# Differential attention heads on one core: three bank pairs for scores, transposes and values one round later, squares per job

## The chip, the cores and the metric

One core of one Trainium2 chip runs the whole program. The metric is the device time of one execution in microseconds (us). A core has TensorE (PE in the profile; its weight loads are PEld), VectorE (DVE), ScalarE (ACT), GpSimd (POOL) and SyncE (SP, which issues most of the DMAs). Each engine works through its own queue in order, and engines are held to one another by semaphores: an instruction may wait until a counter has reached a value, and may raise a counter when it is done.

## The reference, cut to what matters

The program is a stack of layers; the change lies in one of them, the mixer with differential attention (mixer_c), and there in what stands between the projections to q, k and v and the output projection. There are 8 heads, 512 queries, 768 keys (512 latent and 256 context) and two score maps (c = 0, 1) per head, all in fp32:

```
s = einsum('bqhcd,bkhcd->bhcqk', qi, k) * scale          # two maps a head, d = 64
p = softmax(s, axis=-1)
a = p[:, :, 0] - lam * p[:, :, 1]
o = einsum('bhqk,bkhe->bqhe', a, v)                      # e = 128
o = rms_norm(o, subln) * (1 - lam_init)                  # over e, per query and head
return o.reshape(...) @ w_out
```

## The kernel before, in words

The third part of the program runs four stages one after the other on every engine: CIn (projections; L2325), CHeads (the attention; L2444), COut (the norm over e, the transposes and the output projection; L2559) and Moe (experts, whose weights stream in by DMA). A stage's place in the code gives each engine's queue in order; SP issues the expert weights only after the output projection has been added to the residual (the wait on self.before.over(sp) in Moe.sp).

CHeads has 32 jobs, one for each head and block of 128 queries (job n is head n // 4, block n % 4). The order of work on each engine is written out by rounds(): in round n every part (delay, what) gets job n - delay. PSUM (the tile ps) has 8 banks of 512 fp32 columns.

- TensorE (CHeads.pe), round n: the scores of job n (4 matmuls in the source, 2 column segments of 384 for each of the two maps, 8 MATMUL instructions of 64x384 in the trace) into banks 0 and 1 for map 0, 2 and 3 for map 1; then the values of job n - 2 (6 matmuls accumulated, 12 instructions) into bank 6 or 7; then the transposes of job n - 1 (3 into bank 4, 3 into bank 5). All L196 are scores or values, all L202 transposes. The scores wait until both exponentials of job n - 1 are done: they reuse the same banks. The helpers mm and turn4 stand at L192 to L203.
- VectorE (CHeads.dve), round n: the mix of job n - 1 (two reciprocals L2532 and L2533, a product L2535, P0 + factor * P1 over 768 columns L2537), then for each map of job n the row maximum (L2541) and its negative (L2543), then the copy of the first three transposed blocks of job n - 1 (L2548), then the scaled output row of job n - 2 (L2552).
- ScalarE (CHeads.act), round n: the copy of the last three transposed blocks of job n - 1 (L2514), then the two exponentials of job n, 128x768 each (L2521), with their row sums.

After the last job, COut squares the whole of OT at once on ScalarE (L2587), sums the squares (VectorE L2599), takes mean plus eps (L2601), the root (L2589), the reciprocal (L2603) and scales OT at once (L2606). Only then TensorE transposes OT (8 groups of 4, L202), ScalarE (L2592) and VectorE (L2609) take the groups in turn to SBUF with the gain, and OutProj.pe multiplies (L196).

The two waits that order TensorE against the other engines in a round are these:

```
if what == "scores":
    if n:
        pe.wait_ge(self.expd, 2 * n)
...
pe.wait_ge(self.mixed, 4 * n + 4)      # before the transposes of job n
```

Of the kernel before, what the change touches and what calls it, by code (L numbers as in the profile page):

```python
# [2443 lines left out]
class CHeads:  # L2444

    SCALE = 64 ** -0.5

    def __init__(self, K, into):  # L2450
# [3 lines left out]
        self.P = [K.take(T) for _ in range(4)]  # L2454
        self.PT = [K.take(6, 128) for _ in range(2)]
        self.small = [K.take(8) for _ in range(12)]
# [3 lines left out]
        self.pt0, self.pt1 = s["ch_pt0"], s["ch_pt1"]  # L2460

    def scores_at(self, c):
        return self.K.ps[:, 2 * c:2 * c + 2, 0:384]

    def exps(self, n, c):
        return self.P[(2 * n + c) % 4]

    def nums(self, n, c):
        return self.small[(2 * n + c) % 12]

    def rounds(self, parts):

        for n in range(34):
            for delay, what in parts:
                if 0 <= n - delay < 32:
                    yield what, n - delay

    def pe(self, pe):
        K, ps = self.K, self.K.ps
        self.into.over(pe)  # L2480
        for what, n in self.rounds(((0, "scores"), (2, "value"), (1, "turn"))):
            h, qb = divmod(n, 4)
            if what == "scores":
                if n:
                    pe.wait_ge(self.expd, 2 * n)
                for j, (a, w) in enumerate(SEGS):
                    for c in range(2):
                        rows = slice(64 * c, 64 * c + 64)
                        ins = mm(pe, ps[:, 2 * c + j, 0:w], [(self.into.Qs[rows, h, qb * 128:(qb + 1) * 128], self.into.Ks[rows, h, a:a + w])])
                        if j:  # L2490
                            ins.then_inc(self.scored, 1)
            elif what == "value":
                pe.wait_ge(self.pt0, n + 1)
                pe.wait_ge(self.pt1, n + 1)
                if n >= 2:
                    pe.wait_ge(self.out, n - 1)
                mm(pe, ps[:, 6 + n % 2, 0:128], [(self.PT[n % 2][:, kt, :], self.into.VV[:, kt, 128 * h:128 * h + 128]) for kt in range(6)]
                   ).then_inc(self.valued, 1)
            else:
                pe.wait_ge(self.mixed, 4 * n + 4)  # L2500
                for half in range(2):
                    if n:
                        pe.wait_ge((self.pt0, self.pt1)[half], n)
                    turn4(pe, ps[:, 4 + half, :], [self.exps(n, 0)[:, c * 128:(c + 1) * 128] for c in range(3 * half, 3 * half + 3)], K.C("ident")
                          ).then_inc(self.turned, 1)

    def act(self, act):
        ps = self.K.ps
        for what, n in self.rounds(((1, "turned"), (0, "exp"))):
            if what == "turned":  # L2510
                act.wait_ge(self.turned, 2 * n + 2)
                if n >= 2:
                    act.wait_ge(self.valued, n - 1)
                act.activation(self.PT[n % 2][:, 3:6, :], ps[:, 5, 0:384].rearrange("p (c t) -> p c t", t=128), ACT.Copy).then_inc(self.pt1, 1)  # L2514
            else:
                for c in range(2):
                    sm = self.nums(n, c)
                    act.wait_ge(self.max, 4 * n + 2 * c + 2)
                    if n >= 2:
                        act.wait_ge(self.turned, 2 * n - 2)  # L2520
                    act.activation(self.exps(n, c).rearrange("p (s n) -> p s n", n=384), self.scores_at(c), ACT.Exp, bias=sm[:, 0:1],  # L2521
                                   scale=self.SCALE, accum_out=sm[:, 1:2]).then_inc(self.expd, 1)

    def dve(self, dve):
        ps = self.K.ps
        self.into.over(dve)
        for what, n in self.rounds(((1, "mix"), (0, "max"), (1, "turned"), (2, "out"))):
            s0, s1 = self.nums(n, 0), self.nums(n, 1)
            if what == "mix":
                P0, P1 = self.exps(n, 0), self.exps(n, 1)  # L2530
                dve.wait_ge(self.expd, 2 * n + 2)
                dve.reciprocal(s1[:, 1:2], s1[:, 1:2]).then_inc(self.mixed, 1)  # L2532
                dve.reciprocal(s0[:, 2:3], s0[:, 1:2]).then_inc(self.mixed, 1)  # L2533
# [919 lines left out]
```

## Time and profile before

| | |
|---|---|
| median of 3 runs | 4707.38 us (4703.64 to 4708.06) |
| the profiled execution | 4702.54 us, its span 4700.7 us |
| mean granted TensorE clock | 0.91 |
| busy share of the span | PE 84%, PEld 48%, DVE 35%, ACT 28%, POOL 5% |
| the attention of this layer, first score matmul to last output row | 3703.59 to 3925.02 us of the span |
| from there to the first matmul of the output projection | to 3944.93 us |
| costliest lines of the program | L196 PE 1841.9 us busy, L2626 PE 1033.8, L572 PE 463.0 |

The busy shares are averages over a dozen stages with different limits; the stage that the change touches is less than a twentieth of the span. It has to be read by itself: the chain of waits tells which wait ends last there, the timeline how one round goes.

### The profile page before, as it was taken

The page shows a single profiled execution, that of the slowest core. Times are in us where ns is not written, and L with a number is a line of the kernel's source. Part 1 is how long each engine was busy: PE and PEld are TensorE (multiplying, and loading weights), DVE is VectorE, ACT ScalarE, POOL GpSimd, SP SyncE. Part 2 cuts the span into 40 slices and gives each one's busy share as a digit, 9 for nine tenths or more (in the row PEclk, how much of TensorE's full clock was granted, in tenths as well). Part 3 has the DMA queues.
Part 4 walks back from the last instruction along what each step waited for, and adds up shares of the span by engine and source line. Part 5 has one row for each costly group of instructions (what it writes and reads, how often), then busy time and mean ns, then how long its engine had stood idle before and what let it go on. Part 6 is the DMA issues. An engine that isn't in the chain of part 4 may idle for free. (4 is left out here: it accounts for less than half of the span.)

```text
span 4700.7 us, 76675 instructions
## 1 busy us (share of the span) xinstructions
PE 3932.8 (84%) x32256; PEld 2271.8 (48%) x32256; DVE 1628.5 (35%) x4139; ACT 1312.2 (28%) x2871; POOL 227.4 (5%) x221
## 2 busy tenths in 40 slices
PE   5998577777786999998879959999879867699996
PEld 2554466666664546664657643333245444333332
DVE  2001466666672113432365221111132363211112
ACT  2000234444442123324434212222135232122221
POOL 0000000000000000101100010000011000100000
PEclk7999699899997999999868969999989988799998
DMA  5221544443432200002100059999832000699996
GB/s 198 88 73 43 146 114 118 116 114 112 120 107 80 103 10 1 19 19 78 53 1 1 1 186 355 381 382 381 297 130 65 36 1 1 236 382 378 380 377 255
DMA packets 450872, 697.55 MB, mean 148 GB/s; under 512 B 168762, under 2 KB 191448, under 8 KB 450008
## 3 DMA queue, kind: packets, MB, share of 16 engines
q1 hardware_dynamic: 428600, 613.83, 38.0%
q0 software_dynamic: 14752, 53.53, 3.4%
q10 hardware_dynamic: 7168, 25.17, 1.4%
q8 instruction: 261, 4.28, 0.4%
q14 instruction: 91, 0.75, 0.1%
HBM read 625.57 MB, written 64.54 MB: 147 GB/s over the span
## 5 line engine op out<-in xcount | busy, mean ns | idle before, releaser
L196 PE MATMUL ps<-arena 128*128 128x384 f32 (+9 forms) x6718 | 1841.9, 451 | 266.8 <-ACT arena L2521 73.8
L196 PEld LDWEIGHTS ps<-arena 128*128 128x128 f32 (+3 forms) x6718 | 1099.8, 204 | 980.6 <-issue 524.2
L2626 PE MATMUL ps<-arena 128*32 128x512 f32 x9216 | 1033.8, 602 | 47.0 <-DMA arena<-in_w 42.3
L2626 PEld LDWEIGHTS ps<-arena 128*32 128x32 f32 x9216 | 307.0, 110 | 676.0 <-issue 659.3
L572 PE MATMUL ps<-arena 64*64 64x64 f32 (+1 forms) x10624 | 463.0, 241 | 182.0 <-DVE arena L1133 63.2
L572 PEld LDWEIGHTS ps<-arena 64*64 64x64 f32 x10624 | 414.3, 146 | 262.6 <-issue 102.7
L202 PE MATMUL ps<-arena 128*128 128x128 f32 x1248 | 208.2, 308 | 121.6 <-DVE arena L3028 44.5
L2760 DVE COPY arena<-ps 128x384 f32<-128x384 f32 x64 | 35.7, 558 | 675.5 <-PE ps L2685 675.5
L202 PEld LDWEIGHTS ps<-arena 128*128 128x128 f32 x1248 | 167.2, 167 | 138.2 <-DVE arena L3028 47.9
L2736 ACT ACTIVATE arena<-ps 96x512 f32<-96x512 f32 x64 | 38.0, 594 | 650.0 <-PE ps L2626 650.0
L545 DVE SCALAR_TENSOR_TENSOR arena<-arena 128x768 f32<-128x768 f32 x48 | 45.1, 1011 | 350.4 <-PE ps L196 350.4
L386 DVE SCALAR_TENSOR_TENSOR arena<-ps,arena 128x512 f32<-128x512 f32 (+1 forms) x48 | 31.8, 662 | 307.6 <-PE ps L196 307.6
L513 ACT ACTIVATE arena<-ps 128x384 f32<-128x384 f32 x64 | 31.4, 491 | 352.5 <-PE ps L196 352.5
L2778 DVE TENSOR_TENSOR arena<-ps,arena 64x512 f32<-64x512 f32 x64 | 43.7, 682 | 226.4 <-ACT arena L2748 226.4
L1464 DVE TENSOR_REDUCE arena<-ps 128x1 f32<-128x768 f32 x64 | 61.3, 958 | 159.8 <-PE ps L196 159.8
L901 PE MATMUL ps<-arena 64*64 64x64 f32 x2304 | 103.6, 248 | 14.9 <-DVE arena L1215 11.0
L2748 ACT ACTIVATE arena<-ps 64x512 f32<-64x512 f32 x64 | 38.1, 595 | 244.4 <-PE ps L2626 244.4
L330 PE MATMUL ps<-arena 128*128 128x512 f32 (+1 forms) x208 | 87.7, 587 | 20.5 <-ACT arena L321 20.5
L2791 POOL DMA_INDIRECT arena<-htok,arena x64 | 57.8, 904 | 955.5 <-PE ps L2685 948.5
L901 PEld LDWEIGHTS ps<-arena 64*64 64x64 f32 x2304 | 91.2, 160 | 25.3 <-DVE arena L1215 17.3
L247 ACT ACTIVATE arena<-arena 128x768 f32<-128x768 f32 (+1 forms) x32 | 24.5, 785 | 254.8 <-DVE arena L386 254.8
L2541 DVE TENSOR_REDUCE arena<-ps 128x1 f32<-128x768 f32 x64 | 61.0, 953 | 88.8 <-PE ps L196 87.4
(280 smaller groups left out, 3472.8 us busy)
## 6 DMA issues: line engine op xcount, KB each, us to landing
arena<-in_w SPq DMA_DIRECT2D x192, 2048.0 KB, 22.5
arena<-in_w_mod SPq DMA_DIRECT2D x24, 2048.0 KB, 9.0
arena<-in_mod_w SPq DMA_DIRECT2D x12, 2048.0 KB, 15.3
yb<-arena ACTq DMA_DIRECT2D x64, 384.0 KB, 6.3
arena<-in_rwkv_w_in SPq DMA_DIRECT2D x8, 2048.0 KB, 10.6
rkvg<-arena POOLq DMA_DIRECT2D x32, 384.0 KB, 2.6
arena<-rkvg SPq DMA_DIRECT2D x32, 384.0 KB, 4.1
arena<-di SPq DMA_DIRECT2D x192, 64.0 KB, 2.6
```

The lines of the kernel that those rows point to most:

```text
L196: ins = pe.matmul(out, l, r, start=(i == 0), stop=(i == len(pairs) - 1))
L202: ins = pe.transpose(bank[:, i * 128:(i + 1) * 128], src, ident)
L330: ins = pe.matmul(out, w[:, k, :], self.H[:, k, a:a + n], start=(k == 0), stop=(k == KT - 1), skip_group_check=True)
L545: dve.scalar_tensor_tensor(LP[:, k, :], XX[:, k, :], K.PR("mu")[:, 8 * j + k:8 * j + k + 1], H[:, k, :], ALU.mult, ALU.add).then_inc(s["in ...
L572: ins = pe.matmul(out[p, :], l[p, :], r[p, :], start=(i == 0), stop=(i == len(pairs) - 1))
L901: ins = pe.matmul(out[p, :], src[p, :], ident[p, p], start=True, stop=True)
L1464: dve.tensor_reduce(mx, src, AX.XY if masks is None else AX.X, ALU.max).then_inc(self.max, 1)
L2541: dve.tensor_reduce(sm[:, 0:1], self.scores_at(c), AX.XY, ALU.max).then_inc(self.max, 1)
L2626: return pe.matmul(bank[32 * at:32 * at + 32, :], left[:, k, 32 * g:32 * g + 32], right[:, k, :], start=first, stop=last)
L2748: act.activation(YS[0:64, 512:1024], ps[64:128, 7, :], ACT.Copy).then_inc(self.y0, 1)
L2778: dve.tensor_tensor(YS[0:64, 512:1024], ps[0:64, 7, :], YS[0:64, 512:1024], ALU.add).then_inc(self.y1, 1)
L2791: pool.indirect_dma_start(out=moe.HG[i % 3][0:ROWS, :], out_offset=None, in_=self.K.scr["htok"][0:moe.nt, :], in_offset=bass.IndirectOffse ...
```

## The change

Six things are done to CHeads and COut.

- Scores get three pairs of banks, 0 to 5; map c of job n takes pair (2n + c) % 3. Scores of job n wait for 2n - 1 exponentials, where it was 2n.
- The transposes of a job go to banks 6 and 7, columns 0 to 383, and the values to columns 384 to 511 of bank 6 or 7. Transposes of job n now wait, for n > 0, until the transposed copy of job n - 1 (ch_pt) and the output row of job n - 1 (ch_out) are done.
- Transposes come 2 rounds behind the scores (before 1), values 3 (before 2), and the values stand ahead of the scores in TensorE's round. There are 36 rounds, before 34.
- ScalarE takes all six transposed blocks in one copy, behind the exponentials of the round; VectorE's copy (L2548) is gone. VectorE's round is maximum, mix, output row; the two reciprocals are one of two columns.
- ScalarE squares each output row of 128 columns when it is there, 4 rounds behind the scores, with the row sum as accumulator output. The big square and the big sum of COut are gone, the next stage waits for 32 squares.
- COut scales OT in four parts, one for each query block, and TensorE starts to transpose a block when its part is scaled.

The diff, with comments and blank lines cut:

```
--- before.py
+++ after.py
@@ -2445,115 +2445,117 @@
 
 
 
     SCALE = 64 ** -0.5
+    JOBS = 32
 
     def __init__(self, K, into):
         self.K, self.s, self.into = K, K.s, into
         K.top = into.inner
         self.OT = K.take(4, D)
-        self.P = [K.take(T) for _ in range(4)]
+        self.P = [[K.take(T) for _ in range(2)] for _ in range(3)]
         self.PT = [K.take(6, 128) for _ in range(2)]
-        self.small = [K.take(8) for _ in range(12)]
+        self.small = [K.take(8) for _ in range(8)]
+        self.SS, self.junk = K.take(4, 8), K.take(128)
         s = K.s
         self.scored, self.turned, self.valued = s["ch_scored"], s["ch_turned"], s["ch_valued"]
         self.max, self.expd, self.mixed, self.out = s["ch_max"], s["ch_exp"], s["ch_mixed"], s["ch_out"]
-        self.pt0, self.pt1 = s["ch_pt0"], s["ch_pt1"]
-    def scores_at(self, c):
-        return self.K.ps[:, 2 * c:2 * c + 2, 0:384]
-    def exps(self, n, c):
-        return self.P[(2 * n + c) % 4]
-    def nums(self, n, c):
-        return self.small[(2 * n + c) % 12]
+        self.pt, self.squared = s["ch_pt"], s["ch_squared"]
+    def scores_at(self, n, c):
+        b = 2 * ((2 * n + c) % 3)
+        return self.K.ps[:, b:b + 2, 0:384]
+    def values_at(self, n):
+        return self.K.ps[:, 6 + n % 2, 384:512]
+    def rows(self, n):
+        h, qb = divmod(n, 4)
+        return self.OT[:, qb, 128 * h:128 * h + 128]
 
     def rounds(self, parts):
 
-        for n in range(34):
+        for n in range(self.JOBS + 4):
             for delay, what in parts:
-                if 0 <= n - delay < 32:
+                if 0 <= n - delay < self.JOBS:
                     yield what, n - delay
 
     def pe(self, pe):
         K, ps = self.K, self.K.ps
         self.into.over(pe)
-        for what, n in self.rounds(((0, "scores"), (2, "value"), (1, "turn"))):
+        for what, n in self.rounds(((3, "value"), (0, "scores"), (2, "turn"))):
             h, qb = divmod(n, 4)
             if what == "scores":
-                if n:
-                    pe.wait_ge(self.expd, 2 * n)
+                if n >= 1:
+                    pe.wait_ge(self.expd, 2 * n - 1)
                 for j, (a, w) in enumerate(SEGS):
                     for c in range(2):
                         rows = slice(64 * c, 64 * c + 64)
-                        ins = mm(pe, ps[:, 2 * c + j, 0:w], [(self.into.Qs[rows, h, qb * 128:(qb + 1) * 128], self.into.Ks[rows, h, a:a + w])])
+                        ins = mm(pe, self.scores_at(n, c)[:, j, :], [(self.into.Qs[rows, h, qb * 128:(qb + 1) * 128], self.into.Ks[rows, h, a:a + w])])
                         if j:
                             ins.then_inc(self.scored, 1)
             elif what == "value":
-                pe.wait_ge(self.pt0, n + 1)
-                pe.wait_ge(self.pt1, n + 1)
-                if n >= 2:
-                    pe.wait_ge(self.out, n - 1)
-                mm(pe, ps[:, 6 + n % 2, 0:128], [(self.PT[n % 2][:, kt, :], self.into.VV[:, kt, 128 * h:128 * h + 128]) for kt in range(6)]
+                pe.wait_ge(self.pt, n + 1)
+                mm(pe, self.values_at(n), [(self.PT[n % 2][:, kt, :], self.into.VV[:, kt, 128 * h:128 * h + 128]) for kt in range(6)]
                    ).then_inc(self.valued, 1)
             else:
-                pe.wait_ge(self.mixed, 4 * n + 4)
+                pe.wait_ge(self.mixed, 3 * n + 3)
+                if n:
+                    pe.wait_ge(self.pt, n)
+                    pe.wait_ge(self.out, n)
                 for half in range(2):
-                    if n:
-                        pe.wait_ge((self.pt0, self.pt1)[half], n)
-                    turn4(pe, ps[:, 4 + half, :], [self.exps(n, 0)[:, c * 128:(c + 1) * 128] for c in range(3 * half, 3 * half + 3)], K.C("ident")
-                          ).then_inc(self.turned, 1)
+                    ins = turn4(pe, ps[:, 6 + half, :], [self.P[n % 3][0][:, c * 128:(c + 1) * 128] for c in range(3 * half, 3 * half + 3)], K.C("ident"))
+                ins.then_inc(self.turned, 1)
 
     def act(self, act):
         ps = self.K.ps
-        for what, n in self.rounds(((1, "turned"), (0, "exp"))):
+        self.into.over(act)
+        for what, n in self.rounds(((0, "exp"), (2, "turned"), (4, "square"))):
             if what == "turned":
-                act.wait_ge(self.turned, 2 * n + 2)
+                act.wait_ge(self.turned, n + 1)
                 if n >= 2:
                     act.wait_ge(self.valued, n - 1)
-                act.activation(self.PT[n % 2][:, 3:6, :], ps[:, 5, 0:384].rearrange("p (c t) -> p c t", t=128), ACT.Copy).then_inc(self.pt1, 1)
-            else:
+                act.activation(self.PT[n % 2].rearrange("p (j c) t -> p j (c t)", j=2), ps[:, 6:8, 0:384], ACT.Copy).then_inc(self.pt, 1)
+            elif what == "exp":
+                sm = self.small[n % 8]
                 for c in range(2):
-                    sm = self.nums(n, c)
                     act.wait_ge(self.max, 4 * n + 2 * c + 2)
-                    if n >= 2:
-                        act.wait_ge(self.turned, 2 * n - 2)
-                    act.activation(self.exps(n, c).rearrange("p (s n) -> p s n", n=384), self.scores_at(c), ACT.Exp, bias=sm[:, 0:1],
-                                   scale=self.SCALE, accum_out=sm[:, 1:2]).then_inc(self.expd, 1)
-    def dve(self, dve):
-        ps = self.K.ps
-        self.into.over(dve)
-        for what, n in self.rounds(((1, "mix"), (0, "max"), (1, "turned"), (2, "out"))):
-            s0, s1 = self.nums(n, 0), self.nums(n, 1)
-            if what == "mix":
-                P0, P1 = self.exps(n, 0), self.exps(n, 1)
-                dve.wait_ge(self.expd, 2 * n + 2)
-                dve.reciprocal(s1[:, 1:2], s1[:, 1:2]).then_inc(self.mixed, 1)
-                dve.reciprocal(s0[:, 2:3], s0[:, 1:2]).then_inc(self.mixed, 1)
-                dve.wait_ge(self.mixed, 4 * n + 1)
-                dve.tensor_scalar(s1[:, 2:3], s1[:, 1:2], s0[:, 1:2], self.into.lam[:, 4:5], ALU.mult, ALU.mult).then_inc(self.mixed, 1)
-                dve.wait_ge(self.mixed, 4 * n + 3)
-                dve.scalar_tensor_tensor(P0, P1, s1[:, 2:3], P0, ALU.mult, ALU.add).then_inc(self.mixed, 1)
-            elif what == "max":
-                for c, sm in enumerate((s0, s1)):
-                    dve.wait_ge(self.scored, 2 * n + c + 1)
-                    dve.tensor_reduce(sm[:, 0:1], self.scores_at(c), AX.XY, ALU.max).then_inc(self.max, 1)
-                    dve.wait_ge(self.max, 4 * n + 2 * c + 1)
-                    dve.tensor_scalar(sm[:, 0:1], sm[:, 0:1], -self.SCALE, None, ALU.mult).then_inc(self.max, 1)
-            elif what == "turned":
-                dve.wait_ge(self.turned, 2 * n + 1)
-                if n >= 2:
-                    dve.wait_ge(self.valued, n - 1)
-                dve.tensor_copy(self.PT[n % 2][:, 0:3, :], ps[:, 4, 0:384].rearrange("p (c t) -> p c t", t=128)).then_inc(self.pt0, 1)
+                    if n >= 3:
+                        act.wait_ge(self.turned, n - 2)
+                    act.activation(self.P[n % 3][c].rearrange("p (s n) -> p s n", n=384), self.scores_at(n, c), ACT.Exp, bias=sm[:, c:c + 1],
+                                   scale=self.SCALE, accum_out=sm[:, 2 + c:3 + c]).then_inc(self.expd, 1)
             else:
                 h, qb = divmod(n, 4)
+                act.wait_ge(self.out, n + 1)
+                if n:
+                    act.wait_ge(self.squared, n)
+                act.activation(self.junk, self.rows(n), ACT.Square, accum_out=self.SS[:, qb, h:h + 1]).then_inc(self.squared, 1)
+    def dve(self, dve):
+        self.into.over(dve)
+        for what, n in self.rounds(((0, "max"), (1, "mix"), (3, "out"))):
+            sm = self.small[n % 8]
+            if what == "mix":
+                P0, P1 = self.P[n % 3]
+                dve.wait_ge(self.expd, 2 * n + 2)
+                dve.reciprocal(sm[:, 4:6], sm[:, 2:4]).then_inc(self.mixed, 1)
+                dve.wait_ge(self.mixed, 3 * n + 1)
+                dve.tensor_scalar(sm[:, 6:7], sm[:, 5:6], sm[:, 2:3], self.into.lam[:, 4:5], ALU.mult, ALU.mult).then_inc(self.mixed, 1)
+                dve.wait_ge(self.mixed, 3 * n + 2)
+                dve.scalar_tensor_tensor(P0, P1, sm[:, 6:7], P0, ALU.mult, ALU.add).then_inc(self.mixed, 1)
+            elif what == "max":
+                for c in range(2):
+                    dve.wait_ge(self.scored, 2 * n + c + 1)
+                    dve.tensor_reduce(sm[:, c:c + 1], self.scores_at(n, c), AX.XY, ALU.max).then_inc(self.max, 1)
+                    dve.wait_ge(self.max, 4 * n + 2 * c + 1)
+                    dve.tensor_scalar(sm[:, c:c + 1], sm[:, c:c + 1], -self.SCALE, None, ALU.mult).then_inc(self.max, 1)
+            else:
                 dve.wait_ge(self.valued, n + 1)
-                dve.tensor_scalar(self.OT[:, qb, 128 * h:128 * h + 128], ps[:, 6 + n % 2, 0:128], s0[:, 2:3], None, ALU.mult).then_inc(self.out, 1)
+                dve.tensor_scalar(self.rows(n), self.values_at(n), sm[:, 4:5], None, ALU.mult).then_inc(self.out, 1)
 
     def over(self, e):
-        e.wait_ge(self.out, 32)
-        e.wait_ge(self.pt1, 32)
+        e.wait_ge(self.squared, self.JOBS)
 
 
 class COut:
@@ -2561,7 +2563,6 @@
 
     def __init__(self, K, into, heads):
         self.K, self.s, self.into, self.heads = K, K.s, into, heads
-        self.SQ, self.r = K.take(4, D), K.take(32)
         self.O = K.take(KT, TX)
         free = (K.s["c_mm"], 36)
         self.proj = OutProj(K, "c", K.I["w_out_c"], self.O, K.MODS[3], 16, ((0, 0, TX),), (free, free))
@@ -2572,9 +2573,9 @@
     def pe(self, pe, sums):
         K, s = self.K, self.s
         self.heads.over(pe)
-        pe.wait_ge(s["c_sub"], 4)
         for i in range(8):
             qb, c = divmod(i, 2)
+            pe.wait_ge(s["c_sub"], 3 + qb)
             turn4(pe, K.ps[:, i, :], [self.heads.OT[:, qb, m * 128:(m + 1) * 128] for m in range(4 * c, 4 * c + 4)], K.C("ident")
                   ).then_inc(s["c_out_turned"], 1)
         for c in range(2):
@@ -2582,11 +2583,9 @@
         self.proj.pe(pe, sums)
 
     def act(self, act, sums):
-        K, s = self.K, self.s
-        self.heads.over(act)
-        act.activation(self.SQ, self.heads.OT, ACT.Square).then_inc(s["c_sub_act"], 1)
-        act.wait_ge(s["c_sub"], 2)
-        act.activation(self.r, self.r, ACT.Sqrt).then_inc(s["c_sub_act"], 1)
+        K, s, SS = self.K, self.s, self.heads.SS
+        act.wait_ge(s["c_sub"], 1)
+        act.activation(SS, SS, ACT.Sqrt).then_inc(s["c_sub_act"], 1)
         for qb in range(4):
             act.wait_ge(s["c_out_turned"], 2 * qb + 1)
             act.activation(self.O[:, 0:4, qb * 128:(qb + 1) * 128], K.ps[:, 2 * qb, :].rearrange("p (k t) -> p k t", k=4), ACT.Copy,
@@ -2594,16 +2593,15 @@
         self.proj.act(act, sums)
 
     def dve(self, dve):
-        K, s, r, sub = self.K, self.s, self.r, self.s["c_sub"]
+        K, s, SS, sub = self.K, self.s, self.heads.SS, self.s["c_sub"]
+        self.heads.over(dve)
+        dve.tensor_scalar(SS, SS, 1.0 / 128, 1e-6, ALU.mult, ALU.add).then_inc(sub, 1)
         dve.wait_ge(s["c_sub_act"], 1)
-        dve.tensor_reduce(r.unsqueeze(2), self.SQ.rearrange("p q (h n) -> p (q h) n", h=8), AX.X, ALU.add).then_inc(sub, 1)
-        dve.wait_ge(sub, 1)
-        dve.tensor_scalar(r, r, 1.0 / 128, 1e-6, ALU.mult, ALU.add).then_inc(sub, 1)
-        dve.wait_ge(s["c_sub_act"], 2)
-        dve.reciprocal(r, r).then_inc(sub, 1)
-        dve.wait_ge(sub, 3)
-        rows = self.heads.OT.rearrange("p q (h n) -> p (q h) n", h=8)
-        dve.tensor_tensor(rows, rows, r.unsqueeze(2).broadcast_to([128, 32, 128]), ALU.mult).then_inc(sub, 1)
+        dve.reciprocal(SS, SS).then_inc(sub, 1)
+        dve.wait_ge(sub, 2)
+        for qb in range(4):
+            rows = self.heads.OT[:, qb, :].rearrange("p (h n) -> p h n", h=8)
+            dve.tensor_tensor(rows, rows, SS[:, qb, :].unsqueeze(2).broadcast_to([128, 8, 128]), ALU.mult).then_inc(sub, 1)
         for qb in range(4):
             dve.wait_ge(s["c_out_turned"], 2 * qb + 2)
             dve.tensor_scalar(self.O[:, 4:8, qb * 128:(qb + 1) * 128], K.ps[:, 2 * qb + 1, :].rearrange("p (k t) -> p k t", k=4),
```

## Rows read from the trace of the kernel before

**Rows 1.** The chain of waits, in order of time, one round (start us, us, what):

```profile
3803.34 3.10 PE ps L196 x20
3806.44 0.67 PE ps L202 x6
...
3807.52 1.88 ACT arena L2521 x4
```

**Rows 2.** The timeline, same stretch (start us, us, engine line op):

```profile
3803.32 0.16 DVE L2532 RECIPROCAL arena<-arena 128x1 f32<-128x1 f32 x1 [1.65 <-ACT arena L2521]
...
3803.52 0.27 DVE L2535 TENSOR_SCALAR arena<-arena 128x1 f32<-128x1 f32 x1
3803.83 1.02 DVE L2537 SCALAR_TENSOR_TENSOR arena<-arena 128x768 f32<-128x768 f32 x1
...
3804.93 0.96 DVE L2541 TENSOR_REDUCE arena<-ps 128x1 f32<-128x768 f32 x1
...
3807.06 0.56 DVE L2548 COPY arena<-ps 128x384 f32<-128x384 f32 x1
...
3807.53 0.34 DVE L2552 TENSOR_SCALAR arena<-ps,arena 128x128 f32<-128x128 f32 x1
...
3809.44 4.56 PE L196 MATMUL ps<-arena 64*128 64x384 f32 x20 [2.35 <-ACT arena L2521]
...
3812.40 0.96 DVE L2541 TENSOR_REDUCE arena<-ps 128x1 f32<-128x768 f32 x1 [1.46 <-PE ps L196]
```

**Rows 3.** The waits between 3704 and 3925 us (total, times, longest):

```profile
ACT arena L2514 <- PE ps L202: 142.6, 32, 5.5
...
PE ps L196 <- ACT arena L2521: 73.8, 31, 3.4
```

**Rows 4.** Stretches: an earlier attention stage, then this one (PEclk, DMA share, GB/s last):

```profile
2342.00:2474.00 132.00, 101.98 (x505) 80.65 (x505) 84.70 (x331) 44.73 (x143) 0.00 (x0) 0.63 0.00 1
3726.00:3917.00 191.00, 125.81 (x729) 84.50 (x729) 122.07 (x280) 62.72 (x141) 0.00 (x0) 0.87 0.00 1
```

**Rows 5.** The timeline of the last job and of what follows it:

```profile
3916.96 1.57 PE L196 MATMUL ps<-arena 128*128 128x128 f32 x12 [0.63 <-DVE arena L2548]
...
3919.16 1.02 DVE L2537 SCALAR_TENSOR_TENSOR arena<-arena 128x768 f32<-128x768 f32 x1
...
3920.24 0.88 PE L202 MATMUL ps<-arena 128*128 128x128 f32 x6 [1.71 <-DVE arena L2537]
...
3921.15 0.49 ACT L2514 ACTIVATE arena<-ps 128x384 f32<-128x384 f32 x1 [2.53 <-PE ps L202]
...
3921.74 2.89 PE L196 MATMUL ps<-arena 128*128 128x128 f32 x12 [0.63 <-DVE arena L2548]
3924.67 0.35 DVE L2552 TENSOR_SCALAR arena<-ps,arena 128x128 f32<-128x128 f32 x1 [3.03 <-PE ps L196]
3925.05 3.62 ACT L2587 ACTIVATE arena<-arena 128x4096 f32<-128x4096 f32 x1 [3.41 <-DVE arena L2552]
3928.69 1.28 ACT L2589 ACT_TABLE_LOAD   x1
3928.70 4.42 DVE L2599 TENSOR_REDUCE arena<-arena 128x32 f32<-128x4096 f32 x1 [3.68 <-ACT arena L2587]
...
3934.02 4.42 DVE L2606 TENSOR_TENSOR arena<-arena 128x4096 f32<-128x4096 f32 x1
...
3940.57 0.75 DVE L2609 TENSOR_SCALAR arena<-ps,arena 128x512 f32<-128x512 f32 x1 [2.12 <-PE ps L202]
...
3944.93 13.97 PE L196 MATMUL ps<-arena 128*128 128x512 f32 x32 [0.89 <-ACT arena L2592]
```

**Rows 6.** The chain of waits behind the output projection:

```profile
4006.74 1.28 ACT L227
...
4008.03 0.69 ACT arena L227
```

**Rows 7.** The DMA queue's waits, 3700 to 4300 us:

```profile
SPq L2931 <- DVE arena L386: 302.2, 1, 302.2
```

## The prediction

> **What bounds the kernel now.** I read the chain of waits first, because a stage that is a twentieth of the span can't be judged by busy shares. In the loop it repeats the same four steps in every round [rows 1]: 20 matmuls (scores of one job, values of an earlier one) 3.10 us, 6 transposes 0.67, the ScalarE copy of 0.49, two exponentials 1.88, and the next scores. The listing of waits says it from the other side [rows 3]: TensorE waits 31 times for the exponentials, 73.8 us in all, ScalarE 32 times for the transposes. VectorE's maxima and its mix lie beside the matmuls and are not on the chain. So a round is one loop through TensorE and ScalarE: from 3803.34 to 3809.44, 6.10 us [rows 1, 2]. The next round begins with TensorE at its lower level, the same 20 matmuls take 4.56 [rows 2], and it lasts 7.56. The mean is 221.4 us (3703.59 to 3925.02, from the table of times) over 32 jobs, 6.9. The granted clock in the loop is 0.87, so 26% of the time is spent at 1.2 GHz in place of 2.4 [rows 4].
>
> **The new round, step by step.** What matters is which counter each part waits for, so I follow round r. TensorE: values of job r-3, scores of r, transposes of r-2. VectorE: maxima of r, mix of r-1, output row of r-3. ScalarE: exponentials of r, copy of r-2, square of r-4.
> - The transposes of job r-2 wait for ch_out = r-2, that is for the output row of job r-3. VectorE does that row in the same round r, behind the maxima of r and the mix of r-1. And the maxima need the scores of r. So what was beside the chain now stands in it. Behind the waiting transposes, on TensorE, are the values and the next scores.
> - The values of r-2 stand ahead of the scores of r+1 and wait for the copy of r-2, which ScalarE makes after those transposes. So the scores of r+1 can't start early, whatever the third pair of banks allows.
>
> The loop is then: scores, maxima, mix, output row, transposes, copy, values, scores. The exponentials of r (about 2.2 after the first maximum starts) are done before the transposes and drop out of the chain. At TensorE's full level:
> - scores to the first maximum: 3803.34 to 3804.93, 1.59 [rows 1, 2];
> - two maxima with their negatives: 3804.93 to 3807.06, 2.13 [rows 2];
> - mix: 3803.32 to 3804.93 is 1.61, one reciprocal (some 0.08 of issue) less, 1.53 [rows 2];
> - output row 0.34 [rows 2], hand-over to TensorE 0.05 (3920.18 to 3920.24 is such a one, [rows 5]);
> - six transposes until ScalarE starts: 3920.24 to 3921.15, 0.91 [rows 5];
> - the copy of 768 columns: not in the trace. Not below the 0.49 of 384 columns [rows 5], not above two of them, 0.98; an exponential of that shape with its sum is 0.94 [rows 1]. I take 0.85 with hand-over;
> - values: 12 instructions 1.57 to the end of the last [rows 5], of which the last one's drain lies under the next group, so 1.33; with 0.06 of hand-overs.
>
> Sum 8.80 us. The upper bound of the copy adds 0.13 a round, some 4 us in all, the lower takes 12 off; letting the values last 1.57 adds 7.
>
> At the lower level scores take 3809.44 to 3812.40, 2.96 [rows 2]; values 2.89 against 1.57, so 1.32 more [rows 5]; six transposes, at half of that difference, 0.66 more. That is 3.35 more, with rounding 12.2 us a round.
>
> **Fill and drain.** 36 rounds are not all alike. In rounds 0 and 1 nothing waits for values: scores wait for the first exponential of the job before, 1.59 + 1.15 + 1.00 and hand-overs, 3.8 each. Round 2 takes 7.0 (scores, both maxima, second exponential, copy, values). Then 28 full rounds bring the scores of job 31. Behind these come one round of about 8.8 and two short ones of some 3.8 (row, transposes, copy, values), and the last row and its square, 17.4. At the full level: 14.6 + 28 x 8.80 + 17.4 = 278.4. At the lower: 20.6 + 28 x 12.2 + 25.5 = 387.7.
>
> **Which clock.** The trace has this loop at 0.87 and an earlier attention stage at 0.63, with no DMA in either [rows 4]; 0.63 is 74% of the time at the lower level. TensorE rests 2.35 us once a round now [rows 2]. In the new round it rests 4.05 and then 0.9 of 8.8. That is a longer rest and a smaller part of the time at work than now, so I take the row on that side, 0.63: 278.4 + 0.74 x 109.3 = 359.3 us, 11.3 a full round. Against 221.4 that is +137.9.
>
> The Trainium skill ("TensorE: Matmul & The Clock Gate", HAM oscillation) says that a loop whose bursts are parted by long waits falls back to the lower level at every wait; by that the attention would take 387.7. Here the trace agrees only in part: the present loop falls back in every second round.
>
> **Copies, squares, banks.** The VectorE copy that goes (0.56, of which 0.47 until the next) was off the chain and is worth nothing. The square of 128 columns is hidden: ScalarE has two exponentials, one copy and it, under 3.4 of 8.8 us. If that cover went, it would cost its own length, below 0.6, a round. No table load stood between the last copy and the big Square [rows 5], so I expect none in the loop.
>
> **COut.** Before: 3925.02 to 3944.93, 19.9 us [rows 5]. Gone are the square (3.62) and the sum (4.42). Left, counted from the last small square: the table load 1.28; mean, root and reciprocal, which with their waits were 5.35 - 4.42 = 0.93, of which the mean lies beside the load, 0.7; four parts of 4.42 / 4 = 1.11, 4.4, with TensorE transposing beside them; then VectorE's four copies at 0.75 and hand-over [rows 5], 3.3. Sum 9.7, so 10.2 us less.
>
> The Trainium skill ("ScalarE: Activation LUTs", What ACT_TABLE_LOAD costs) counts 1.38 us of drain on top of the 1.28 of a load. By it COut would save 8.8. The trace doesn't show that: the activation follows its load at once, 4006.74 + 1.28 to 4008.03 [rows 6].
>
> **What follows** shifts as a whole. The DMA queue stands still until the output projection has been added (302.2 us of waiting, [rows 7]), so the expert weights can't hide anything.
>
> Net +137.9 - 10.2 = +127.7 on the profiled 4702.5: 4830. The median of the three runs lies 4.8 above that execution, so 4835.
>
> **Rivals.**
> - *All at the lower level.* TensorE falls back in every wait and never recovers in its 5.6 us burst. For: the longer rest. Against: in the present loop one burst at the lower level is followed by the full one. 387.7 - 221.4 - 10.2 = +156.1: 4864. Chance 0.2.
> - *Clock as now, 0.87.* Values and scores stand together in one burst of 2.9 us, which might hold the level. 306.8, so +75.2: 4783; with no lower level at all +46.8, 4754. Chance 0.15.
> - *Faster.* The wait of the transposes for the output row decides. If it found its number already there, the transposes would run under the maxima, and if the copy then were early enough for the values, nothing but VectorE's own 4.0 us (2.13 + 1.53 + 0.34) would bound a round: 35 x 4.1 = 144, with COut -88: 4620. It decides from the point where row r-3 is done before the maxima of r begin. VectorE's order of the parts speaks against it, since the row stands behind both. Even with that wait alone gone, ScalarE's order (exponentials, then copy) leaves 1.59 + 2.13 + 1.1 + 0.85 + 1.33 = 7.0 a round, no gain. Chance 0.04.
> - *The change does less than it says*: small gaps hide more than I think and the round comes out near 7. Chance 0.01.
>
> **The numbers.** The forecast has 0.6: clock between 0.55 and 0.75. Its own range, with the copy's and values' bounds, is 4805 to 4855. Taking in the lower level throughout and most of the 0.87 case gives 4770 to 4868, which leaves out under 2 in 10. A difference under 0.2% (9 us) can't be told from none. Slower by more than that: 0.95; within it 0.01; faster 0.04.
>
> **What would show it.** Right: scores to scores 11 to 12 us with two lengths; VectorE's output row ends just before the transposes start; TensorE's wait ended by L-line of the output row, 4 us, 30 times; a second wait for the ScalarE copy, some 0.9; ScalarE idle for more than half; from the last row to the projection about 10 us; granted clock near 0.6. Wrong: TensorE starts the transposes before the mix of the round is done (my reading of the counters fails); the copy is longer than 1 us; table loads inside the loop; or the clock stays above 0.8, which alone takes 50 us off.

## The result, and the profile after

The changed kernel takes 4802.95 us (median of 4 runs, 4797.54 to 4811.46) against 4707.72 for the kernel before (4703.64 to 4710.42): ratio 1.0205, 95% interval 1.0187 to 1.0222. It is 95 us slower. The point forecast was 4835, the range 4770 to 4868.

The profiled execution has a span of 4795.7 us against 4700.7. Where the 95.0 us are is read from four marks on the timeline: the first score matmul, the end of the last output row, the first matmul of the output projection, the end of the span.

| stretch | before | after | difference |
|---|---|---|---|
| start to first score matmul | 3703.59 | 3699.76 | -3.8 |
| first scores to end of last output row | 221.4 | 328.9 | +107.4 |
| from there to the output projection | 19.9 | 10.8 | -9.1 |
| output projection to the end | 755.8 | 756.2 | +0.5 |

So nothing upstream or downstream gives back or adds more than 4 us, and what follows the output projection has moved as a whole.

The chain of waits of the changed kernel, in order of time (start us, us, what), one round; it answers to [rows 1]:

```profile
3796.75 0.95 DVE arena L2550
...
3797.88 0.87 DVE arena L2550
...
3799.35 1.02 DVE arena L2546
...
3800.77 0.86 PE ps L202 x6
...
3801.66 0.82 ACT arena L2519
...
3802.52 4.47 PE ps L196 x20
3806.99 0.95 DVE arena L2550
```

The maxima (L2550), the mix (L2546) and the copy (L2519) are in the chain, where before it had only matmuls, a copy and exponentials. From one first maximum to the next it is 10.24 us. The exponentials are gone from it. The timeline of the same stretch, which answers to [rows 2], shows the queues (start us, us, engine line op, idle before and releaser):

```profile
3796.73 0.96 DVE L2550 TENSOR_REDUCE arena<-ps 128x1 f32<-128x768 f32 x1 [6.35 <-PE ps L196]
...
3797.80 0.95 DVE L2550 TENSOR_REDUCE arena<-ps 128x1 f32<-128x768 f32 x1
...
3798.96 0.90 ACT L2526 ACTIVATE arena<-ps,arena 128x768 f32<-128x768 f32 x1
...
3799.35 1.02 DVE L2546 SCALAR_TENSOR_TENSOR arena<-arena 128x768 f32<-128x768 f32 x1
...
3800.28 0.35 DVE L2555 TENSOR_SCALAR arena<-ps,arena 128x128 f32<-128x128 f32 x1
...
3800.77 0.84 PE L202 MATMUL ps<-arena 128*128 128x128 f32 x6 [4.07 <-DVE arena L2555]
3801.66 0.81 ACT L2519 ACTIVATE arena<-ps 128x768 f32<-128x768 f32 x1 [1.70 <-PE ps L202]
...
3802.52 4.42 PE L196 MATMUL ps<-arena 128*128 128x128 f32 x20 [0.90 <-ACT arena L2519]
...
3806.97 0.96 DVE L2550 TENSOR_REDUCE arena<-ps 128x1 f32<-128x768 f32 x1 [6.34 <-PE ps L196]
```

The output row (L2555) ends at 3800.63, the transposes (L202) begin at 3800.77 after 4.07 us of rest, the copy of 768 columns takes 0.81, and 20 matmuls take 4.42. The waits between 3704 and 4030 us (total, times, longest), against [rows 3]:

```profile
DVE arena L2550 <- PE ps L196: 191.8, 31, 8.4
ACT arena L2526 <- DVE arena L2552: 164.8, 31, 7.1
...
PE ps L202 <- DVE arena L2555: 115.1, 30, 4.1
...
PE ps L196 <- ACT arena L2519: 31.1, 32, 3.2
```

TensorE's 31 waits for exponentials (73.8 us) have become 30 waits for the output row (115.1 us) and 32 for the copy (31.1 us). Stretches of the changed kernel (us, busy times, then PEclk, DMA share and GB/s), the first for the early rounds, the second for the steady ones, against [rows 4]:

```profile
3726.00:3765.00 39.00, 24.08 (x92) 16.70 (x91) 11.26 (x24) 9.26 (x21) 0.00 (x0) 0.64 0.00 0
3768.00:3985.00 217.00, 111.22 (x546) 83.62 (x546) 80.08 (x170) 65.33 (x149) 0.00 (x0) 0.83 0.00 0
3792.30:3795.20 2.90, 2.90 (x14) 2.67 (x14) 0.00 (x0) 0.22 (x2) 0.00 (x0) 0.51 0.00 0
3795.20:3796.70 1.50, 1.50 (x9) 0.63 (x8) 0.00 (x0) 0.00 (x0) 0.00 (x0) 1.00 0.00 0
3796.70:3801.60 4.90, 0.83 (x6) 0.64 (x6) 3.75 (x8) 1.98 (x4) 0.00 (x0) 1.00 0.01 2
```

The early rounds last 11.4 to 12.3 us at a granted clock of 0.64. Of the 31 distances from first maximum to first maximum, the last 23 are 10.23 or 10.24, at 0.83, and the lower level, a third of the time, always lies on the same piece: the first 2.9 us of the 20 matmuls run at 1.2 GHz (0.51 in the row), the last 1.5 at 2.4. TensorE's long rest of 4.07 us and the six transposes behind it still stand at the full level (1.00 from 3796.70 to 3801.60); it falls in the short rest for the copy. Behind the loop (timeline of the changed kernel, against [rows 5]):

```profile
4028.27 0.35 DVE L2555 TENSOR_SCALAR arena<-ps,arena 128x128 f32<-128x128 f32 x1 [3.53 <-PE ps L196]
4028.65 0.31 ACT L2533 ACTIVATE arena<-arena 128x128 f32<-128x128 f32 x1 [1.30 <-DVE arena L2555]
...
4029.07 1.28 ACT L2588 ACT_TABLE_LOAD   x1
...
4030.36 0.23 ACT L2588 ACTIVATE arena<-arena 128x32 f32<-128x32 f32 x1
...
4031.01 4.63 DVE L2604 TENSOR_TENSOR arena<-arena 128x1024 f32<-128x1024 f32 x4
...
4032.38 6.17 PE L202 MATMUL ps<-arena 128*128 128x128 f32 x32 [4.16 <-DVE arena L2604]
...
4039.44 13.97 PE L196 MATMUL ps<-arena 128*128 128x512 f32 x32 [0.89 <-ACT arena L2591]
```

These are the last output row and its square (L2533), the table load, the root 0.01 us behind it, four scaled parts in 4.63 us with the transposes beside them, and the projection at 4039.44.

### The profile page after: what moved, and what is told of

It reads as the page before. It is cut to its first block and busy times, and to the rows that moved or that the text cites. A ratio compares the mean times of both kernels' runs of the same rounds, so it can differ in the third digit from the quotient of the medians.

```text
span 4795.7 us, 76643 instructions
## 1 busy us (share of the span) xinstructions
PE 3954.0 (82%) x32256; PEld 2296.7 (48%) x32256; DVE 1604.4 (33%) x4077; ACT 1335.2 (28%) x2934; POOL 227.1 (5%) x221
## 5 line engine op out<-in xcount | busy, mean ns | idle before, releaser
L196 PEld LDWEIGHTS ps<-arena 128*128 128x128 f32 (+3 forms) x6718 | 1127.3, 209 | 920.3 <-issue 500.4
L202 PE MATMUL ps<-arena 128*128 128x128 f32 x1248 | 211.9, 312 | 231.8 <-DVE arena L2555 115.1
L202 PEld LDWEIGHTS ps<-arena 128*128 128x128 f32 x1248 | 167.8, 168 | 266.7 <-DVE arena L2546 132.1
L2550 DVE TENSOR_REDUCE arena<-ps 128x1 f32<-128x768 f32 x64 | 61.0, 953 | 257.5 <-PE ps L196 257.5
L2526 ACT ACTIVATE arena<-ps,arena 128x768 f32<-128x768 f32 x64 | 57.7, 901 | 169.8 <-DVE arena L2552 167.9
```

Source lines behind the costliest of these rows:

```text
L196: ins = pe.matmul(out, l, r, start=(i == 0), stop=(i == len(pairs) - 1))
L202: ins = pe.transpose(bank[:, i * 128:(i + 1) * 128], src, ident)
L2526: act.activation(self.P[n % 3][c].rearrange("p (s n) -> p s n", n=384), self.scores_at(n, c), ACT.Exp, bias=sm[:, c:c + 1], scale=self.SCA ...
L2550: dve.tensor_reduce(sm[:, c:c + 1], self.scores_at(n, c), AX.XY, ALU.max).then_inc(self.max, 1)
```

## The experiments

All compare with runs of the kernel before on the same chip (4709.64 us median in the first four, 4703.94 in the last two). Marks on the timeline are those of the table above.

**1. The output row first on VectorE.** In CHeads.dve of the changed kernel:

```diff
-        for what, n in self.rounds(((0, "max"), (1, "mix"), (3, "out"))):
+        for what, n in self.rounds(((3, "out"), (0, "max"), (1, "mix"))):
```

> One edit to the changed kernel: VectorE's output row of job r-3 stands ahead of the maxima of job r instead of behind the mix. My theory (the transposes wait for that row, and the row waited for the maxima of the same round) expects the transposes to start right after the scores, and the loop to be scores 1.59, two maxima 2.13, the second exponential 1.1, the copy 0.85, values 1.33, which is 7.0 us a round at the full level in place of 8.7. The whole attention comes to about 265 us at a granted clock near 0.8, so 4740 us (4720 to 4765). The rival (the round is long because one ScalarE copy of 768 columns, or the shared banks 6 and 7, are slow) expects no change: 4803.

Measured: 4744.01 us (4740.70 to 4759.08), ratio to before 1.0088 (1.0063 to 1.0113), 59 us below the changed kernel. Its timeline:

```profile
3791.60 0.35 DVE L2555 TENSOR_SCALAR arena<-ps,arena 128x128 f32<-128x128 f32 x1 [3.31 <-PE ps L196]
...
3793.11 0.87 PE L202 MATMUL ps<-arena 128*128 128x128 f32 x6
3793.21 0.96 DVE L2550 TENSOR_REDUCE arena<-ps 128x1 f32<-128x768 f32 x1 [1.26 <-PE ps L196]
...
3795.45 0.90 ACT L2526 ACTIVATE arena<-ps,arena 128x768 f32<-128x768 f32 x1
...
3796.34 0.80 ACT L2519 ACTIVATE arena<-ps 128x768 f32<-128x768 f32 x1
...
3797.19 3.24 PE L196 MATMUL ps<-arena 128*128 128x128 f32 x16 [3.21 <-ACT arena L2519]
...
3801.74 0.96 DVE L2550 TENSOR_REDUCE arena<-ps 128x1 f32<-128x768 f32 x1 [2.50 <-PE ps L196]
```

The row is done at 3791.95 and the transposes follow the scores with no rest; rounds alternate between some 8.50 and 8.58 us, in place of 10.24. TensorE now rests 3.21 us for the copy, which stands behind the exponentials on ScalarE, as the loop worked out beforehand has it; the granted clock from 3740 to 3900 is 0.81. The order of three parts in VectorE's queue was worth 1.7 us a round.

**2. The copy first on ScalarE.** In CHeads.act of the changed kernel:

```diff
-        for what, n in self.rounds(((0, "exp"), (2, "turned"), (4, "square"))):
+        for what, n in self.rounds(((2, "turned"), (0, "exp"), (4, "square"))):
```

> One edit to the changed kernel: ScalarE's copy of job r-2 stands ahead of the exponentials of job r. My theory expects no change, 4803 us (4793 to 4813): the copy waits for the transposes, which wait for the output row, and by then the exponentials are long done, so their order doesn't matter. The rival (the copy queued behind the exponentials holds the values back, which is what the order on ScalarE suggests) expects 1 to 2 us less a round, 4745 to 4775.

Measured: 4798.70 us (4789.90 to 4803.43), ratio to before 1.0192 (1.0169 to 1.0216), against 1.0205 of the changed kernel: no difference that could be told. The rounds are 10.24 as before and TensorE's rest ahead of the transposes is 4.07 us. Alone this order is worth nothing.

**3. Both.** The two edits together.

> Both edits together: output row first on VectorE, copy first on ScalarE. By my theory only the two together untie the loop, since either wait is enough to hold it: transposes follow the scores at once, the copy follows them while VectorE is at the maxima, values follow the copy, and the next scores need only the first exponential. The loop is then near 4.4 to 5 us at the full level, bounded by the scores, transposes, copy and values in turn and by VectorE's own 4.0. The attention comes to 150 to 195 us depending on the clock, the program to 4655 us (4625 to 4690), under both kernels. The rival (each edit gives its own share, so both give their sum) expects about 4740, and contention on the banks 4700 or more.

Measured: 4634.18 us (4627.79 to 4641.90), ratio 0.9839 (0.9819 to 0.9859): 75 us under the kernel before, 169 under the changed one, where the parts alone gave 59 and 4. The timeline:

```profile
3761.01 0.87 PE L202 MATMUL ps<-arena 128*128 128x128 f32 x6
3761.11 0.96 DVE L2550 TENSOR_REDUCE arena<-ps 128x1 f32<-128x768 f32 x1 [0.90 <-PE ps L196]
3761.92 0.81 ACT L2519 ACTIVATE arena<-ps 128x768 f32<-128x768 f32 x1 [1.94 <-PE ps L202]
...
3762.78 3.10 PE L196 MATMUL ps<-arena 128*128 128x128 f32 x20 [0.90 <-ACT arena L2519]
...
3764.66 0.34 DVE L2555 TENSOR_SCALAR arena<-ps,arena 128x128 f32<-128x128 f32 x1
...
3765.81 0.87 PE L202 MATMUL ps<-arena 128*128 128x128 f32 x6
```

From the third on every round lasts 4.80 us. Transposes, copy and values follow one another while VectorE does the maxima, TensorE rests 0.90 us a round, for the copy, and the granted clock from 3720 to 3840 is 1.00. The loop is now values and scores (3.03 to the transposes), transposes 0.91, copy 0.86.

**4. TensorE's rest filled.** In CHeads.pe of the changed kernel, behind the scores; the result of these matmuls is overwritten:

```diff
+                if n >= 3:
+                    for _ in range(4):
+                        mm(pe, self.values_at(n), [(K.C("ident"), self.into.VV[:, kt, 0:128]) for kt in range(4)])
```

> The changed kernel with work added: behind the scores of each job from 3 on, 16 more fp32 matmuls of 128x128 (identity times a part of the values, written where the values of that job pair go later and overwritten by them), some 3.5 us of TensorE a round, inside its rest of 4.07. If the rest is what brings TensorE to its lower level, and the lower level costs the 1.55 us by which the 20 matmuls take 4.47 and not 2.92, the round goes from 10.24 to 8.7 to 8.9 although there is more work: about 4755 us (4745 to 4775). The rival (the level is not set by that rest, or the burst is slow for another reason) expects 4803 or more, since the added work can then only delay the transposes.

Measured: 4757.06 us (4746.41 to 4769.96), ratio to before 1.0108 (1.0079 to 1.0137), 46 us below the changed kernel, with 32 more MATMUL instructions in each of 29 rounds. Stretch and timeline of the filled kernel:

```profile
3768.00:3960.00 192.00, 165.46 (x1248) 137.31 (x1247) 81.14 (x174) 67.49 (x154) 0.00 (x0) 1.00 0.00 1
```

```profile
3802.12 0.96 DVE L2553 TENSOR_REDUCE arena<-ps 128x1 f32<-128x768 f32 x1 [5.02 <-PE ps L196]
...
3805.68 0.35 DVE L2558 TENSOR_SCALAR arena<-ps,arena 128x128 f32<-128x128 f32 x1
...
3806.17 0.85 PE L202 MATMUL ps<-arena 128*128 128x128 f32 x6 [0.31 <-DVE arena L2558]
3807.05 0.81 ACT L2522 ACTIVATE arena<-ps 128x768 f32<-128x768 f32 x1 [1.70 <-PE ps L202]
...
3807.92 4.30 PE L196 MATMUL ps<-arena 128*128 128x128 f32 x29 [0.90 <-ACT arena L2522]
...
3811.04 0.96 DVE L2553 TENSOR_REDUCE arena<-ps 128x1 f32<-128x768 f32 x1 [5.02 <-PE ps L196]
```

Rounds are 8.92 us, the rest ahead of the transposes 0.31, the clock 1.00. The chain is the same as in the changed kernel, row, transposes, copy, values and scores, and only the last of them is shorter: from the first value matmul to the first maximum 3.12 us (3807.92 to 3811.04) in place of 4.45 (3802.52 to 3806.97). So 1.3 us a round of the slowdown was the lower level, and TensorE's rest had brought it.

**5. The third pair of banks made useless.** In the kernel of experiment 3:

```diff
-                    pe.wait_ge(self.expd, 2 * n - 1)
+                    pe.wait_ge(self.expd, 2 * n)
```

> The kernel with both edits (row first, copy first, 4634 us), and the third pair of banks made useless: the scores of job n wait for 2n exponentials again, as in the kernel before, and not for 2n - 1. In that kernel's timeline the scores of a round start 1.33 us behind the values, at 3764.11, and the second exponential ends at 3764.49. So my theory expects the scores 0.4 to 0.5 us later in each round, 13 to 16 us in all: 4648 us (4643 to 4655). The rival (with the queues in the right order the third pair is worth nothing, or it was what made the gain) expects 4634 or more than 4680.

Measured: 4647.84 us (4639.06 to 4654.06), ratio 0.9874 (0.9859 to 0.9889), 14 us above experiment 3 by these medians of two sets of runs. Against the kernel before in its own set it is 56 us faster, where experiment 3 was 75; the intervals of 0.9839 and 0.9874 touch. In the traces, first scores to projection is 170.2 us with the third pair and 183.0 without. But the steady round is 5.03, only 0.23 longer, where 0.4 to 0.5 was expected. The 1.33 for the values in the expectation is the reason: with the third pair the transposes start at 3765.81, and scores need 1.49 up to there (in this kernel 3761.48 to 3762.97), so the scores really start at 3764.32 and an exponential that ends at 3764.49 holds them by 0.2. Over 28 rounds that is 6.4 us.

The rest, another 6.4, is in the first three rounds, 5.28, 6.24 and 7.38 against 3.90, 3.81 and 4.81. Of it 2.0 us is the wait itself: in the first two of these rounds TensorE rests 3.38 and 3.30 us for the second exponential, where with the third pair it rests 2.41 and 2.25 for the first. The other 4.4 goes with the level: the granted clock is 0.50 from 3719 to 3732 here and 1.00 in the other kernel. Whether the third pair is what keeps it up isn't shown. The kernel of experiment 2 has it, rests the same 2.41 us, and yet its next scores ran at the lower level (granted 0.52 from 3707 to 3709) and its first rounds took 5.27, 4.03 and 7.29. So 8.4 of the 12.8 us are the wait, and the rest may fall otherwise in another run. That the time came out at the 4648 us of the expectation is in part luck.

**6. The squares and the four parts alone.** The kernel before with this added to CHeads.act, one round more for it, and COut taken from the changed kernel, which waits for the 32 squares:

```diff
-        for what, n in self.rounds(((1, "turned"), (0, "exp"))):
+        for what, n in self.rounds(((1, "turned"), (0, "exp"), (3, "square"))):
...
+            elif what == "square":
+                h, qb = divmod(n, 4)
+                act.wait_ge(self.out, n + 1)
+                if n:
+                    act.wait_ge(self.squared, n)
+                act.activation(self.junk, self.OT[:, qb, 128 * h:128 * h + 128], ACT.Square, accum_out=self.SS[:, qb, h:h + 1]).then_inc(self.squared, 1)
```

> The kernel before with one part of the change alone: squares of each output row on ScalarE, 3 rounds behind the scores and last in its round, no big square and no big sum, OT scaled in four parts and transposed part by part. The loop before has ScalarE idle 3.8 us a round ahead of its copy, so the squares (0.30 + 0.19 us) cost nothing there. My theory expects the stretch from the last output row to the output projection at 10.4 to 10.8 us in place of 19.9, so 9 to 9.5 us less: ratio 0.998 to the kernel before, and the loop's round lengths as they were. The rival (the squares in the loop put off the exponentials, 0.5 us a round) expects 6 us more or no difference.

Measured: 4691.61 us (4682.49 to 4697.22, 8 runs), ratio 0.9967 (0.9957 to 0.9978), 12 us by the medians. The trace has the stretch behind the last row at 9.9 us in place of 19.9, somewhat less than the 10.4 to 10.8 expected, and the steady rounds, from maximum to maximum, in pairs of 6.19 and 7.47, the same 13.66 for two as in the kernel before, whose 6.10 and 7.56 were taken from scores to scores. Its timeline in the loop:

```profile
3802.35 0.90 ACT L2528 ACTIVATE arena<-ps,arena 128x768 f32<-128x768 f32 x1
...
3803.22 0.31 ACT L2521 ACTIVATE arena<-arena 128x128 f32<-128x128 f32 x1
...
3803.39 3.10 PE L196 MATMUL ps<-arena 64*128 64x384 f32 x20 [2.35 <-ACT arena L2528]
...
3807.18 0.49 ACT L2515 ACTIVATE arena<-ps 128x384 f32<-128x384 f32 x1 [3.55 <-PE ps L202]
```

The next scores begin at 3803.39 beside the square, and ScalarE still rests 3.55 us ahead of its copy. This part of the change is a gain by itself.

## Why the prediction was right or wrong

**Direction and mechanism: right.** The round was read off the counters as scores, maxima, mix, output row, transposes, copy, values, scores, and the chain after has these eight pieces in this order. From the first maximum to the transposes the forecast was 4.05 (2.13 + 1.53 + 0.34 + 0.05) and the trace has 4.04 (3796.73 to 3800.77). Six transposes: 0.91 forecast, 0.89 measured. The copy: 0.85 with hand-over forecast, 0.86 measured. Experiments 1 to 3 show that both waits hold the loop, each by itself: freeing the copy alone gives nothing, freeing the row alone leaves ScalarE's order to hold it, and only both untie it. The rival that a wait not met would give 4620 was priced close: with both orders turned the kernel is at 4634, and the loop at 4.80 rather than 4.1.

**The row alone: right, but for the clock.** With this wait alone gone the round was to be 7.0 at the full level and no gain over before. In experiment 1 the piece from the first maximum to the values measures 3.98 (3793.21 to 3797.19; forecast 2.13 + 1.1 + 0.85). Values and scores take 4.55 from there (3797.19 to 3801.74), against 3.12 at the full level in the filled kernel, and that makes the 8.5 at a clock of 0.81. So there is indeed no gain, 1.0088.

**The clock: the step that failed.** I took 0.63, 74% of the time at the lower level, because the rest is longer and the share of work smaller than in the loop before. The early rounds did have it, 0.64, with 11.4 to 12.3 us a round against the 11.3 forecast. Then the round settled at 10.24 and 0.83: a third of the time at the lower level and not three quarters, all on one piece of the burst, while the transposes (1.53 in the early rounds) are back at 0.86. So it costs 1.3 us a round (10.24 against the 8.92 of the filled kernel) and not 2.5. That is the miss: the forecast had 28 full rounds of 11.3, 316.4 us; they measure 293.9 (12.28, 11.43, 12.28, 11.52, 10.90 and 23 of 10.24), and fill and drain 35.4 in place of 42.9, for the same reason. (Over the full level the 28 rounds cost 44 us here, 293.9 less 28 x 8.92, where 316.4 less 28 x 8.80 had 70.) Together 30 us: the attention with its last square grew by 107.9 where 137.9 was forecast. The rival with the clock as now had 4783 and the likeliest case 4835; the truth lies between them, in the stated range of 4770 to 4868 but 2 us below the 4805 to 4855 that the likeliest case gave itself. Two signs that the prediction named came out against its clock: one length of round in place of two, and a granted clock that stays above 0.8, priced at 50 us where the time came out 32 lower. The 0.63 was the row of another stage. No row read from the trace before says where in the longer round the level would fall; the loop before does show that a pattern can repeat, 6.10 and 7.56 in turn.

The Trainium skill's rule on loops with long waits ("TensorE: Matmul & The Clock Gate", HAM oscillation), which would have had all of it at the lower level, is borne out in that every burst of 20 matmuls in the steady loop begins at 1.2 GHz, and not in that it stays there: the last 1.5 us of the same burst are at 2.4. Experiment 4 agrees with its other half, that a loop without the rest stays at the full level.

**The values were too cheap.** I put 12 value matmuls at 1.33 so that values and scores came to 2.92, or 2.98 with the 0.06 of hand-overs. At the full level they measure 3.12 in the filled kernel (and 3.13 in experiment 3, 3762.78 to 3765.91). That is 0.14 a round, 4 us, within the bound of 1.57 that the text kept. The full-level round is 8.92 in experiment 4, against 8.80 forecast, and its whole attention takes 283.3 us to the last row, against the 278.4 forecast with its square.

**COut: right in its parts, 0.7 us off.** Forecast 9.7 from the last small square, measured 10.4 (4029.05 to 4039.44). The scaled parts take 4.63 together, not 4.42, and TensorE was late with its last groups: VectorE's last copies came as a pair of 1.62 after 0.75 us of waiting. The transposes ran at the lower level for most of their time (granted 0.50 from 4031 to 4037), which the forecast had left out; how much of the 0.7 is theirs isn't shown. Experiment 6, where the level is back at 1.00 before the transposes end (1.00 from 3933 on), needs 9.9 us from the last row to the projection in place of 10.8. It shows the saving without the new loop, 10.0 us. The table load stood as forecast: 4029.07 + 1.28, root at 4030.36. The drain of 1.38 us that the Trainium skill ("ScalarE: Activation LUTs", What ACT_TABLE_LOAD costs) adds doesn't appear; by it the root would be at 4031.7.

**Squares and the copy dropped from VectorE: nothing**, as forecast. A square is 0.30 + 0.19 us behind the copy, with ScalarE idle before the copy and after the square, and no table load stood in the loop. Experiment 6 bears out the squares; for the VectorE copy it rests on its place beside the chain, since no run drops it alone. **Downstream: rigid**, +0.5 us.

## What to carry to other kernels

When work is put a round later, look not only at the delays but at where each part stands in its engine's queue: a wait for an old job is as late as whatever is queued ahead of the part that ends it, here the maxima of the newest job. Write the loop of one round down from the counters and add it up; two waits that each close a loop hide one another, so that here one edit gave nothing, the other 59 us and both together 169. Ask of each part that frees another engine (the output row, the copy) whether it can stand first in its round.

## What the runs showed of the hardware that was not expected

- A loop can keep a fixed pattern with TensorE's clock: 23 rounds of 10.23 to 10.24 us, each with the lower level on the first 2.9 us of the same matmuls, after eight uneven ones, the fill among them. The kernel with only the copy moved comes to the same 10.24. In experiment 1 single rounds vary from 8.48 to 8.60, but each two in a row come to 17.07 to 17.09, as two of the kernel before come to 13.65 or 13.66 once it is steady. A constant round by itself is no sign of it (4.80 and 8.92 in experiments 3 and 4, at 1.00), and no run shows why the pattern has just these lengths.
- The level did not fall in the long rest, nor on the transposes right behind it, but about 5 us after the rest began, and the matmuls that paid for it are the next burst.
- More work made the kernel faster: 32 matmul instructions a round whose result is thrown away took 46 us off, with TensorE at 2.4 GHz (granted 1.00 from 3768 to 3960).
